# Preparing the output weights' combinations in eight smaller pieces, with their transfers on ScalarE's queue, and two reordered places on VectorE

## The chip, the cores and the metric

The kernel runs on one core of a Trainium2 chip. The metric is the device time of one launch in microseconds (us), lower is better; each version is timed several times and the median is taken. The core has five engines with an instruction queue each: TensorE (PE in the rows; its weight loads are PEld), VectorE (DVE), ScalarE (ACT), GpSimd (POOL) and SyncE (SP). Each works its queue in order; they meet at semaphores. Transfers between the memory outside the core (HBM) and its on-chip memory are issued on the queues of SP, ACT or POOL and carried by 16 shared DMA engines.

## The reference

A hybrid decoder block on 1024 tokens (plus 16 learned meta tokens) of width 1024, all in float32:

```python
h = rms_norm(z, norm_w[l])
p = (h @ w_in[l] + b_in[l])                     # 1024 -> 8 x 1024
q, fz, iv, g_hg, u, g_pool, m_hg, m_pool = split(p, 8)
o    = rms_norm(hgrn2_chunkwise(q, k, iv, log_f))
y_hg = (o * silu(g_hg)) @ w_down_hg[l]
y_pool = (mixed * pool_scale[l] * silu(g_pool)) @ w_down_pool[l]   # mixed: pooled windows @ pool_w
merged = sigmoid(m_hg) * y_hg + sigmoid(m_pool) * y_pool
z = z + merged @ w_out[l]
out = rms_norm(z, final_norm_w)
```

What matters here are the big matrix products, `h @ w_in`, the two `w_down` products, `merged @ w_out`, and the preparation of the weights `w_out`.

## The kernel before

**Products.** Every 1024-wide matrix product is cut into pairs of 128-column weight blocks, numbered p = 0 to 43. One pair is computed Strassen-Winograd fashion: seven products i = 0 to 6 instead of eight, written here as (p, i). One product is twelve matmuls (L1596): each float32 operand is split into a high part (`w_hi`, `r_hi`, made by ScalarE) and a low part (`w_lo`, `r_lo`, made by VectorE), and high x high, high x low and low x high are summed over four blocks of 128. TensorE takes the products in a fixed order, and three waits recur inside a pair: product (p, 4) needs the bank copied by `copy_second`, (p, 5) needs the copy by `copy_fifth` (ScalarE), and (p, 6) needs `add_22` (VectorE), the quarter that the fifth product ends. (p, 2) needs `copy_first`.

**Who does what beside a product.** For ScalarE and VectorE the function `during(p, i)` lists what they do beside product (p, i): ScalarE copies a bank, applies a sigmoid to a finished quarter (`extra`, L1064) and makes the high part of the weights three products ahead (`high`, L910). VectorE adds a quarter (`add_11` L1957, `add_22` L1966, `add_12` L1973), makes the low part three products ahead (`ahead`, L1872), and at i = 5 sums the next pair's weights (`weight_sums`, L1902 to L1907). All are written by hand in program order, so an instruction that waits holds everything behind it on its engine.

**Stages.** Pairs 26 and 27 (P_MM) and 28 to 31 (P_MH) make the merge gates; pairs 32 to 35 (P_DH) and 36 to 39 (P_DP) are the two down products; 40 to 43 the output product. At 31 to 32 and 35 to 36 the shared operand changes: seven operands (`r_hi`, `r_lo`, 128 x 2048 each) are replaced while products still run. VectorE's order there is the hand-written function `change(f)`: sums over the staged tiles (`stage_sum`, L2452 to L2463), low parts (`operand_low`, L2443) and the usual work. The staged tiles (`stage`) come back from HBM by four 1 MB transfers per change, issued on ScalarE's queue (`load_stage`, L1308).

**The w_out combinations.** The output product too is of the Winograd form, so four sums and differences of blocks of `w_out` have to be made (V5, V7, V6, V4). This is done ahead, during pairs 27 to 30, in one buffer `comb` of four views of 128 x 512: GpSimd issues the load of a piece (L828), VectorE makes the four sums (`comb_sums`, L2382 to L2388, in two parts after two neighbouring products, by the table `COMB_AT`), GpSimd issues the store (L833), then the next load, which waits for the store to have landed. There are four pieces of 1 MB. Load and store are placed by `COMB_DMA` between GpSimd's stores of finished gates (`store_spill`, L798). The first load waits for the last stores of the pooling part (`side_area_free`: semaphores `c_stored`). `stage_sum` of V5 at (30, 3) writes over `comb` and waits until all four pieces are stored. The buffer's memory is shared with the tile of V5.

Of the kernel before, what the change touches and what calls it, by code (L numbers as in the profile page):

```python
# [12 lines left out]
P = 128  # L13
# [40 lines left out]
def pair_table():  # L54
# [6 lines left out]
    for g in range(4):  # L61
# [76 lines left out]
COMB_AT = {(P_MM + 1, 3): (0, 0), (P_MM + 1, 4): (0, 1), (P_MH, 1): (1, 0), (P_MH, 2): (1, 1),  # L138
           (P_MH + 1, 0): (2, 0), (P_MH + 1, 1): (2, 1), (P_MH + 1, 6): (3, 0), (P_MH + 2, 0): (3, 1)}
COMB_DMA = {(P_MM, 3): -1, (P_MM + 1, 0): 0, (P_MH, 0): 1, (P_MH, 3): 2, (P_MH + 1, 3): 3}  # L140
# [45 lines left out]
def hybrid_block(nc, x, meta, norm_w, wstream, pool_w, b_in, lb_logits, hg_norm_w, pool_scale, final_norm_w, out):  # L186
    names = ExitStack()
    with names:
# [15 lines left out]
            "comb_loaded", "comb_made", "comb_stored", "out_loaded0", "out_loaded1", "out_loaded2", "out_loaded3", "out_loaded4", "out_loaded5",  # L204
# [137 lines left out]
        comb = at("comb", [P, 4, HALF], F32, work + 4 * 8192)  # L342
# [47 lines left out]

        third_begun = (S["third_begun0"], S["third_begun1"])
# [181 lines left out]
        def _(sp):  # L573
# [38 lines left out]
            def load_gate(u):  # L612

                n, t = QUARTERS[u % 4]
                after(sp, S["part_made"], u - 1)
                sp.wait_ge(spill_stored[u % 4], 16 * STORES_OF[P_MH + u // 4, u % 4])
                sp.dma_start(gate_in[u % 2][:, :], gate_dram[MH][2 * (u // 4) + n, t]).then_inc(g_loaded[u % 2], 16)
# [19 lines left out]
            def load_slot(slot):  # L637
# [5 lines left out]
                else:  # L643
                    ins = sp.dma_start(dst.rearrange("p (b k) c -> p b (k c)", b=2),
# [42 lines left out]
        def _(pool):  # L687
# [132 lines left out]
            out_blocks = wstream[2 * N_PAIRS:2 * N_PAIRS + 8].rearrange("(b s) p c -> s p b c", s=2)  # L820

            def load_comb(k):

                if k == 0:
                    side_area_free(pool)
                else:
                    pool.wait_ge(S["comb_stored"], 16 * k)
                pool.dma_start(comb[:, :, :], out_blocks[k // 2][:, :, k % 2 * HALF:(k % 2 + 1) * HALF]) \  # L828
                    .then_inc(S["comb_loaded"], 16)

            def store_comb(k):
                pool.wait_ge(S["comb_made"], k + 1)
                pool.dma_start(comb_dram[:, k // 2].rearrange("b p c -> p b c")[:, :, k % 2 * HALF:(k % 2 + 1) * HALF],  # L833
                             comb[:, :, :]).then_inc(S["comb_stored"], 16)
# [1969 lines left out]
```

## Time and profile before

| what | us |
|---|---|
| median of 3 runs | 1050.41 (1050.28 to 1050.82) |
| the profiled execution | 1051.89 |
| its span, first to last instruction | 1050.2 |
| TensorE busy, matmuls | 1018.8 (97%) |
| VectorE busy | 811.9 (77%) |
| ScalarE busy | 510.6 (49%) |
| GpSimd busy | 106.1 (10%) |
| moved by DMA | 117.17 MB, mean 112 GB/s |

Times in rows are from the start of the span. A busy share of 97% leaves little idle time on TensorE, and what there is lies in a few places, so the view to read is TensorE's own timeline: a row there is a run of matmuls with its start, its length, and in brackets how long the engine was idle before it and who released it. A row of the other engines reads the same way.

### The profile page before, as it was taken

The page shows a single profiled execution, that of the slowest core. Times are in us where ns is not written, and L with a number is a line of the kernel's source. Part 1 is how long each engine was busy: PE and PEld are TensorE (multiplying, and loading weights), DVE is VectorE, ACT ScalarE, POOL GpSimd, SP SyncE. Part 2 cuts the span into 40 slices and gives each one's busy share as a digit, 9 for nine tenths or more (in the row PEclk, how much of TensorE's full clock was granted, in tenths as well). Part 3 has the DMA queues.
Part 4 walks back from the last instruction along what each step waited for, and adds up shares of the span by engine and source line. Part 5 has one row for each costly group of instructions (what it writes and reads, how often), then busy time and mean ns, then how long its engine had stood idle before and what let it go on. Part 6 is the DMA issues. An engine that isn't in the chain of part 4 may idle for free.

```text
span 1050.2 us, 18526 instructions
## 1 busy us (share of the span) xinstructions
PE 1018.8 (97%) x7204; PEld 828.9 (79%) x7204; DVE 811.9 (77%) x1319; ACT 510.6 (49%) x860; POOL 106.1 (10%) x170
## 2 busy tenths in 40 slices
PE   7999999999999999999999999999899999999996
PEld 7767888888888888878888887787677888778885
DVE  7989787878787869696676776865468879978975
ACT  7764636363636363644353333443337536435664
POOL 6200000000000101020101001011111011000130
PEclk9999999999999999999999999999999999999999
DMA  7221111111110202121312122135773393568374
GB/s 275 51 81 62 42 61 42 62 42 61 39 64 29 74 23 81 41 101 32 101 55 96 54 78 100 51 125 197 261 293 96 120 351 128 210 204 309 84 164 125
DMA packets 40582, 117.17 MB, mean 112 GB/s; under 512 B 4752, under 2 KB 4752, under 8 KB 40496
## 3 DMA queue, kind: packets, MB, share of 16 engines
q1 hardware_dynamic: 23680, 70.33, 20.4%
q0 software_dynamic: 11152, 34.65, 10.1%
q10 hardware_dynamic: 5664, 11.02, 3.0%
q8 instruction: 57, 0.93, 0.4%
q14 instruction: 29, 0.24, 0.1%
HBM read 86.62 MB, written 29.36 MB: 110 GB/s over the span
## 4 chain that ended last, share of the span: by engine, by line
PE 61%; issue 18%; DVE 13%; DMA 4%; ACT 1%; POOL 1%; SPq 0%; ACTq 0%; DVEq 0%; POOLq 0%
PE acc L1596 49%; DMA comb<-in_wstream 2%; PE levels L1649 2%; DVE r_lo L2443 1%; DVE w_lo L1872 1%; PE miscs L1671 1%; PE miscs L1682 1%; PE miscs L1683 1%; PE acc L1538 1%; DVE att L2029 1%; PE levels L1596 1%; DVE qx L2048 1%; POOL c_spill L818 1%; DMA pt_in<-part_spill 1%; PE miscs L1689 1%
## 5 line engine op out<-in xcount | busy, mean ns | idle before, releaser
L1596 PE MATMUL acc<-r_hi,w_hi 128*128 128x512 f32 x1200 | 333.3, 399 | 11.0 <-ACT fifth L1000 3.4
L1596 PE MATMUL acc<-r_lo,w_hi 128*128 128x512 f32 x1200 | 329.2, 393 | 0.9 <-DVE r_lo L2443 0.8
L1596 PE MATMUL acc<-r_hi,w_lo 128*128 128x512 f32 x1200 | 323.0, 391 | 3.3 <-DVE w_lo L1872 3.3
L1596 PEld LDWEIGHTS acc<-r_hi,w_hi 128*128 128x128 f32 x1200 | 218.2, 188 | 61.7 <-ACT fifth L1000 4.9
L1596 PEld LDWEIGHTS acc<-r_hi,w_lo 128*128 128x128 f32 x1200 | 225.5, 188 | 52.4 <-DVE w_lo L1872 4.2
L1596 PEld LDWEIGHTS acc<-r_lo,w_hi 128*128 128x128 f32 x1200 | 223.6, 188 | 54.7 <-issue 4.9
L910 ACT ACTIVATE w_hi<-sum 128x512 fp32r<-128x512 f32 x164 | 102.8, 628 | 167.9 <-DVE sum L1905 86.0
L1872 DVE TENSOR_TENSOR w_lo<-sum,w_hi 128x512 fp32r<-128x512 f32 x164 | 111.8, 686 | 47.9 <-ACT w_hi L910 47.4
L1872 DVE TENSOR_TENSOR w_lo<-raws,w_hi 128x512 fp32r<-128x512 f32 x120 | 81.9, 686 | 45.7 <-ACT w_hi L910 45.6
L910 ACT ACTIVATE w_hi<-raws 128x512 fp32r<-128x512 f32 x120 | 74.3, 623 | 21.8 <-PE acc L1596 19.1
L1000 ACT ACTIVATE second<-acc,bias 128x512 f32<-128x512 f32 x31 | 21.2, 684 | 57.8 <-PE acc L1596 57.7
L782 POOL TENSOR_TENSOR o_rs<-o_ms,minus_half 128x8 f32<-128x8 f32 x8 | 16.0, 2003 | 306.9 <-DVE o_ms L2128 306.9
L1000 ACT ACTIVATE first<-acc,bias 128x512 f32<-128x512 f32 x32 | 22.1, 690 | 35.1 <-PE acc L1596 35.1
L1000 ACT ACTIVATE fifth<-acc,bias 128x512 f32<-128x512 f32 x31 | 21.3, 686 | 29.9 <-PE acc L1596 29.5
L2443 DVE TENSOR_TENSOR r_lo<-stage,r_hi 128x2048 fp32r<-128x2048 f32 x14 | 32.0, 2284 | 1.1 <-ACT r_hi L1329 1.1
L1907 DVE TENSOR_TENSOR sum<-sum,raws 128x512 f32<-128x512 f32 x38 | 26.3, 692 | 1.3
L818 POOL DMA_DIRECT2D c_spill<-pg x16 | 8.6, 539 | 179.7 <-DVE pg L2375 179.2
L1329 ACT ACTIVATE r_hi<-stage 128x2048 fp32r<-128x2048 f32 x14 | 26.8, 1913 | 0.0
L1905 DVE TENSOR_TENSOR sum<-sum,raws 128x512 f32<-128x512 f32 x38 | 26.0, 685 | 0.0
L1903 DVE TENSOR_TENSOR sum<-raws 128x512 f32<-128x512 f32 x38 | 26.0, 685 | 0.0
L1902 DVE TENSOR_TENSOR sum<-raws 128x512 f32<-128x512 f32 x38 | 26.0, 685 | 0.0
L1683 PE MATMUL miscs<-vv,att 128*128 128x128 f32 x128 | 24.7, 275 | 0.0
(314 smaller groups left out, 1311.2 us busy)
## 6 DMA issues: line engine op xcount, KB each, us to landing
raws<-in_wstream SPq DMA_DIRECT2D x80, 512.0 KB, 3.7
xin<-in_x SPq DMA_DIRECT2D x8, 512.0 KB, 6.2
a_spill<-gt POOLq DMA_DIRECT2D x16, 256.0 KB, 3.5
c_spill<-pg POOLq DMA_DIRECT2D x16, 256.0 KB, 2.7
comb<-in_wstream POOLq DMA_DIRECT2D x4, 1024.0 KB, 7.8
comb_spill<-comb POOLq DMA_DIRECT2D x4, 1024.0 KB, 5.5
stage<-a_spill ACTq DMA_DIRECT2D x4, 1024.0 KB, 10.7
smh_spill<-zq POOLq DMA_DIRECT2D x16, 256.0 KB, 6.3
```

The lines of the kernel that those rows point to most:

```text
L910: act.activation(high_of(o), operand(o), ACT.Copy).then_inc(S["w_hi"], 1)
L1000: return act.activation(dst, src, ACT.Identity, bias=b, scale=scale)
L1329: act.activation(r_hi[i][:, :, :], STAGED[i][:, :, :], ACT.Copy).then_inc(S["r_hi"], 1)
L1596: ins = pe.matmul(bank[:, :], weights, moving, start=n == 0 and i in (0, 1, y_first), stop=n == 3 * KH - 1, skip_group_check=True)
L1649: ins = pe.matmul(lev[g * GROUP:(g + 1) * GROUP, c * n:(c + 1) * n], kt[:, META + t.start:META + t.stop], q, start=True, stop=True)
L1683: ins = pe.matmul(dst, att[:, s], vv[:, s], start=False, stop=True)
L1872: dve.tensor_tensor(low_of(o), operand(o), high_of(o).bitcast(F32), ALU.subtract).then_inc(S["w_lo"], 1)
L1902: dve.tensor_tensor(sums[S1][:, :], a21, a22, ALU.add).then_inc(done, 1)
L1903: dve.tensor_tensor(sums[S3][:, :], a11, a21, ALU.add).then_inc(done, 1)
L1905: dve.tensor_tensor(sums[S2][:, :], sums[S1][:, :], a11, ALU.add).then_inc(done, 1)
L1907: dve.tensor_tensor(sums[S4][:, :], sums[S2][:, :], a12, ALU.add).then_inc(done, 1)
L2443: dve.tensor_tensor(r_lo[i][:, :, :], STAGED[i][:, :, :], r_hi[i][:, :, :].bitcast(F32), ALU.subtract) \
```

## The change

- The combinations are made in eight pieces of 512 KB (four views of 128 x 256) in three buffers in place of four pieces in one. Two buffers share the memory of the old one, the third lies where `gate_in` lies later.
- Loads and stores of the pieces move from GpSimd's queue to ScalarE's, at places that the tables `COMB_LOAD` and `COMB_STORE` give: after `during(p, i)` of the product named. A load waits for the store of the piece that had the buffer before it; a store waits for the sums. The sums of a piece are made whole, after one product (`COMB_SUM`).
- The four stage loads for the first change of operand, two at (28, 3) and two at (29, 3) before, are issued singly at (28, 6), (29, 3), (29, 6) and (30, 0). `stage_sum` of V5 and V7 move from (30, 3) and (30, 6) to (30, 1) and (30, 3).
- In `change`, used for both changes of operand, VectorE makes the second low part (`operand_low` of B21) and the next `ahead` before `add_22`, not after it.
- In pair 37 the first merge (`use(P_DP, ...)` of that pair's first quarter) moves from after product 4 to after product 5, so behind `add_22` and `weight_sums`.
- Two waits of SP (the first two loads of `gate_in`, and the loads of the combinations at the end) name the new semaphores.

```diff
+COMB_PIECES = 8
+COMB_BUFFER = (0, 1, 2, 0, 1, 2, 0, 2)
+COMB_LOAD = {(P_MM + 1, 1): 0, (P_MM + 1, 2): 1, (P_MM + 1, 3): 2, (P_MH, 1): 3, (P_MH, 3): 4, (P_MH, 5): 5,
...
+STAGE_LOAD = {(P_MH, 6): 0, (P_MH + 1, 3): 1, (P_MH + 1, 6): 2, (P_MH + 2, 0): 3}
...
-                    if (p, x) in COMB_DMA:
-                        k = COMB_DMA[p, x]
-                        if k >= 0:
-                            store_comb(k)
-                        if k < 3:
-                            load_comb(k + 1)
...
+            def load_comb(k):
+
+                n, turn = COMB_BUFFER[k], comb_turn(k)
+                if k == 0:
+                    side_area_free(act)
+                after(act, comb_stored[n], 16 * turn)
+                act.dma_start(comb[n][:, :, :], out_blocks[k // 4][:, :, comb_columns(k)]).then_inc(comb_loaded[n], 16)
+
+            def store_comb(k):
+                n = COMB_BUFFER[k]
+                act.wait_ge(S["comb_made"], k + 1)
+                act.dma_start(comb_dram[:, k // 4].rearrange("b p c -> p b c")[:, :, comb_columns(k)], comb[n][:, :, :]) \
+                    .then_inc(comb_stored[n], 16)
+
+            def comb_and_stage(p, i):
+
+                if (p, i) in COMB_STORE:
+                    store_comb(COMB_STORE[p, i])
+                if (p, i) in COMB_LOAD:
+                    load_comb(COMB_LOAD[p, i])
+                if (p, i) in STAGE_LOAD:
...
@@ -2500,9 +2522,9 @@
                 add_11(p)
                 ahead(p, 3)
                 use(p, 0)
-                add_22(p)
                 operand_low(f, R_B21)
                 ahead(p, 4)
+                add_22(p)
                 ahead(p, 5)
...
-                    if p == P_DH - 2 and i in (3, 6):
-                        stage_sum(0, R_V5 if i == 3 else R_V7)
+                    if p == P_DH - 2 and i in (1, 3):
+                        stage_sum(0, R_V5 if i == 1 else R_V7)
...
-                elif i == 4:
+                elif i == 5:
                     use(P_DP + 1, 0)
```

The order on VectorE beside (27, 3) to (27, 5), before; `zq_159` is the quarter of `add_22`:

```order
L1872 TENSOR_TENSOR w_lo_88<-raws,w_hi_84 128x512
L2382 TENSOR_TENSOR comb<-comb 128x512
L2383 TENSOR_TENSOR comb<-comb 128x512
L1872 TENSOR_TENSOR w_lo_85<-raws,w_hi_81 128x512
L2386 SCALAR_TENSOR_TENSOR comb<-comb 128x512
L2388 SCALAR_TENSOR_TENSOR comb<-comb 128x512
L1966 SCALAR_TENSOR_TENSOR zq_159<-acc,fifth 128x512
```

and after (line numbers are those of the new file):

```order
L1894 TENSOR_TENSOR w_lo_88<-raws,w_hi_84 128x512
L1894 TENSOR_TENSOR w_lo_85<-raws,w_hi_81 128x512
L2404 TENSOR_TENSOR comb_171<-comb_171 128x256
L2405 TENSOR_TENSOR comb_171<-comb_171 128x256
L2407 SCALAR_TENSOR_TENSOR comb_171<-comb_171 128x256
L2409 SCALAR_TENSOR_TENSOR comb_171<-comb_171 128x256
L1988 SCALAR_TENSOR_TENSOR zq_159<-acc,fifth 128x512
```

The four sums now stand together, one product later, at half the width, still ahead of `add_22`.

ScalarE beside (27, 1) to (27, 5), before; what is in square brackets are the semaphores waited for:

```order
L910 ACTIVATE w_hi_82<-sum_92 128x512 [waits mm_done,sums_made]
L910 ACTIVATE w_hi_83<-sum_93 128x512 [waits mm_done,sums_made]
L1000 ACTIVATE second<-acc,bias 128x512 [waits added,mm_done]
L1064 ACTIVATE zq_158<-zq_158 128x512 [waits added]
L910 ACTIVATE w_hi_84<-raws 128x512 [waits mm_done,raw_loaded1]
L1000 ACTIVATE fifth<-acc,bias 128x512 [waits added,mm_done]
L910 ACTIVATE w_hi_81<-raws 128x512 [waits mm_done,raw_loaded2]
L910 ACTIVATE w_hi_82<-raws 128x512 [waits mm_done,raw_loaded2]
```

and after:

```order
L901 ACTIVATE w_hi_82<-sum_92 128x512 [waits mm_done,sums_made]
L1318 DMA comb_171<-in_wstream 128x4x256 [waits c_stored2,c_stored3,c_stored1,c_stored0]
L901 ACTIVATE w_hi_83<-sum_93 128x512 [waits mm_done,sums_made]
L1318 DMA comb_172<-in_wstream 128x4x256
L991 ACTIVATE second<-acc,bias 128x512 [waits added,mm_done]
L1055 ACTIVATE zq_158<-zq_158 128x512 [waits added]
L901 ACTIVATE w_hi_84<-raws 128x512 [waits mm_done,raw_loaded1]
L1318 DMA comb_173<-in_wstream 128x4x256
L991 ACTIVATE fifth<-acc,bias 128x512 [waits added,mm_done]
L901 ACTIVATE w_hi_81<-raws 128x512 [waits mm_done,raw_loaded2]
L901 ACTIVATE w_hi_82<-raws 128x512 [waits mm_done,raw_loaded2]
L1323 DMA comb_spill<-comb_171 128x4x256 [waits comb_made]
```

Three loads and a store now stand between ScalarE's copies; the first load and every store wait there.

VectorE at the first change of operand, beside (31, 3) to (31, 5), before; `r_lo_67` is the second low part, `zq_159` the quarter of `add_22`:

```order
L1872 TENSOR_TENSOR w_lo_88<-raws,w_hi_84 128x512
L1966 SCALAR_TENSOR_TENSOR zq_159<-acc,fifth 128x512
L2443 TENSOR_TENSOR r_lo_67<-stage_151,r_hi_60 128x2048
L1872 TENSOR_TENSOR w_lo_85<-raws,w_hi_81 128x512
L1872 TENSOR_TENSOR w_lo_86<-raws,w_hi_82 128x512
```

and after:

```order
L1894 TENSOR_TENSOR w_lo_88<-raws,w_hi_84 128x512
L2464 TENSOR_TENSOR r_lo_67<-stage_151,r_hi_60 128x2048
L1894 TENSOR_TENSOR w_lo_85<-raws,w_hi_81 128x512
L1988 SCALAR_TENSOR_TENSOR zq_159<-acc,fifth 128x512
L1894 TENSOR_TENSOR w_lo_86<-raws,w_hi_82 128x512
```

`add_22` now stands behind a 128 x 2048 operation and a 128 x 512 one.

## Rows read from the trace of the kernel before

**Rows 1.** Windows: busy us of each engine, granted clock, DMA share, GB/s

```profile
740.00:765.00 25.00, 20.52 (x80) 16.04 (x79) 11.38 (x19) 8.14 (x15) 3.14 (x5) 0.86 0.76 264
```

**Rows 2.** Timeline of TensorE, 690 to 830: start, length, operation, idle before, releaser

```profile
716.93 1.21 PE L1596 MATMUL acc<-r_hi,w_hi 128*128 128x512 f32 x4 [1.04 <-DVE zq L1966]
...
735.30 1.20 PE L1596 MATMUL acc<-r_hi,w_hi 128*128 128x512 f32 x4 [1.71 <-ACT fifth L1000]
...
752.67 1.07 PE L1596 MATMUL acc<-r_lo,w_hi 128*128 128x512 f32 x4
756.51 2.08 PE L1596 MATMUL acc<-r_hi,w_lo 128*128 128x512 f32 x4 [2.78 <-DVE w_lo L1872]
760.28 2.08 PE L1596 MATMUL acc<-r_hi,w_hi 128*128 128x512 f32 x4 [1.70 <-ACT fifth L1000]
762.16 1.60 PE L1596 MATMUL acc<-r_lo,w_hi 128*128 128x512 f32 x4
763.59 1.07 PE L1596 MATMUL acc<-r_hi,w_lo 128*128 128x512 f32 x4
764.50 1.07 PE L1596 MATMUL acc<-r_hi,w_hi 128*128 128x512 f32 x4
...
785.33 1.20 PE L1596 MATMUL acc<-r_hi,w_hi 128*128 128x512 f32 x4 [1.63 <-DVE zq L1966]
```

**Rows 3.** Timeline of VectorE, the same stretch

```profile
705.82 0.69 DVE L1957 TENSOR_TENSOR zq<-acc,first 128x512 f32<-128x512 f32 x1 [1.55 <-DMA c_spill<-pg]
...
713.05 0.69 DVE L2382 TENSOR_TENSOR comb<-comb 128x512 f32<-128x512 f32 x1 [2.83 <-DMA comb<-in_wstream]
...
731.20 0.69 DVE L2382 TENSOR_TENSOR comb<-comb 128x512 f32<-128x512 f32 x1 [6.52 <-DMA comb<-in_wstream]
...
754.56 0.69 DVE L2382 TENSOR_TENSOR comb<-comb 128x512 f32<-128x512 f32 x1 [11.25 <-DMA comb<-in_wstream]
...
781.78 2.29 DVE L2452 TENSOR_TENSOR stage<-stage,stage 128x2048 f32<-128x2048 f32 x1 [1.64 <-DMA comb_spill<-comb]
```

**Rows 4.** Issues by line, 690 to 800, and their landing: weights (512 KB), stage (1 MB)

```profile
L581 SPq DMA_DIRECT2D raws<-in_wstream x9: 327/328/328, 694.5 to 788.4; - x9
...
DMA to landing us min/median/max: 3.3/5.7/8.7
...
L1308 ACTq DMA_DIRECT2D stage<-a_spill x4: 366/460/541, 733.5 to 758.9; - x4
...
DMA to landing us min/median/max: 6.1/10.7/14.0
```

**Rows 5.** Timeline of ScalarE: two rows of its work

```profile
711.08 0.62 ACT L910 ACTIVATE w_hi<-raws 128x512 fp32r<-128x512 f32 x1
...
734.56 0.69 ACT L1000 ACTIVATE fifth<-acc,bias 128x512 f32<-128x512 f32 x1 [0.28 <-issue]
```

**Rows 6.** Timelines of VectorE and TensorE at the first change of operand

```profile
801.07 0.69 DVE L1872 TENSOR_TENSOR w_lo<-raws,w_hi 128x512 fp32r<-128x512 f32 x1 [1.22 <-ACT w_hi L910]
802.04 0.69 DVE L1966 SCALAR_TENSOR_TENSOR zq<-acc,fifth 128x512 f32<-128x512 f32 x1 [0.28 <-PE acc L1596]
...
804.50 1.07 PE L1596 MATMUL acc<-r_hi,w_hi 128*128 128x512 f32 x4
...
826.80 1.20 PE L1596 MATMUL acc<-r_lo,w_hi 128*128 128x512 f32 x4
```

**Rows 7.** The same two timelines at the second change of operand

```profile
879.78 0.69 DVE L1966 SCALAR_TENSOR_TENSOR zq<-acc,fifth 128x512 f32<-128x512 f32 x1 [0.56 <-issue]
...
882.24 1.07 PE L1596 MATMUL acc<-r_hi,w_hi 128*128 128x512 f32 x4
...
906.35 1.21 PE L1596 MATMUL acc<-r_lo,w_hi 128*128 128x512 f32 x4
```

**Rows 8.** The same two timelines in pair 37

```profile
922.41 0.69 DVE L2479 TENSOR_TENSOR mm<-mm,sp_in 128x512 f32<-128x512 f32 x1 [1.26 <-DMA pt_in<-part_spill]
...
924.49 1.19 PE L1596 MATMUL acc<-r_hi,w_hi 128*128 128x512 f32 x4 [0.58 <-DVE mm L1966]
```

More of the change, by code:

```diff
@@ L339, in hybrid_block @@
         m = [mm[:, n, :] for n in range(NK)]
-        comb = at("comb", [P, 4, HALF], F32, work + 4 * 8192)
+        comb = [at(f"comb{n}", [P, 4, HALF // 2], F32, place)
+                for n, place in enumerate((work + 4 * 8192, work + 4 * 8192 + 4096, side + 8192))]
         out_sums = [at(f"out_sum{n}", [P, HALF], F32, ring_at + RING * 4096 + 2048 * n) for n in range(4)]
@@ L389, in hybrid_block @@
         comb_dram = nc.dram_tensor("comb_spill", [4, 2, P, D], F32, kind="Internal").ap()
+        comb_loaded = tuple(S[f"comb_loaded{n}"] for n in range(3))
+        comb_stored = tuple(S[f"comb_stored{n}"] for n in range(3))
         third_begun = (S["third_begun0"], S["third_begun1"])
@@ L643, in load_slot @@
                 else:
+                    for n in range(3):
+                        sp.wait_ge(comb_stored[n], 16 * COMB_BUFFER.count(n))
                     ins = sp.dma_start(dst.rearrange("p (b k) c -> p b (k c)", b=2),
@@ L1309, in load_stage, with comb_columns, comb_turn @@
                     .then_inc(stage_loaded[n // 2], 16)
+            out_blocks = wstream[2 * N_PAIRS:2 * N_PAIRS + 8].rearrange("(b s) p c -> s p b c", s=2)
+            def comb_columns(k):
+                lo = k % 4 * (HALF // 2)
+                return slice(lo, lo + HALF // 2)
+            def comb_turn(k):
+                return COMB_BUFFER[:k].count(COMB_BUFFER[k])
+            def load_comb(k):
[15 more added lines that the diff above has]
+                if (p, i) in STAGE_LOAD:
+                    if STAGE_LOAD[p, i] == 0:
+                        for x in range(4):
+                            act.wait_ge(spill_stored[x], 16 * STORES_OF[P_MM, x])
+                    load_stage(0, STAGE_LOAD[p, i])
             for p in range(P_POOL, P_MH):
@@ L1333, in _ @@
                     during(p, i)
-                    if p in (P_MH, P_MH + 1) and i == 3:
-                        if p == P_MH:
-                            side_area_free(act)
-                            for x in range(4):
-                                act.wait_ge(spill_stored[x], 16 * STORES_OF[P_MM, x])
-                        load_stage(0, 2 * (p - P_MH))
-                        load_stage(0, 2 * (p - P_MH) + 1)
-                    elif p in (P_DH - 1, P_DP - 1) and i in (1, 2, 4, 5):
+                    comb_and_stage(p, i)
+                    if p in (P_DH - 1, P_DP - 1) and i in (1, 2, 4, 5):
                         operand_high((p + 1 - P_DH) // 4, i - 1 if i < 3 else i - 2)
@@ L2375, in mixed, with comb_sums @@
                 dve.tensor_tensor(v, mix_banks[k], v, ALU.mult).then_inc(S["c_made"], 1)
-            def comb_sums(k, part):
-                v5_, v4_, v7_, v6_ = (comb[:, n, :] for n in range(4))
-                dve.wait_ge(S["comb_loaded"], 16 * k + 16)
-                if part == 0:
-                    steps.mark(dve.tensor_tensor(v5_, v5_, v7_, ALU.subtract))
-                    steps.mark(dve.tensor_tensor(v7_, v6_, v7_, ALU.subtract))
-                    return
+            def comb_sums(k):
+                n = COMB_BUFFER[k]
+                v5_, v4_, v7_, v6_ = (comb[n][:, v, :] for v in range(4))
+                dve.wait_ge(comb_loaded[n], 16 * (COMB_BUFFER[:k].count(n) + 1))
+                steps.mark(dve.tensor_tensor(v5_, v5_, v7_, ALU.subtract))
+                steps.mark(dve.tensor_tensor(v7_, v6_, v7_, ALU.subtract))
                 steps.settle()
```

36 lines of the change are left out of this document (15 added, 21 removed).

## The prediction, made before the changed kernel ran

> **What bounds the kernel now.** I read TensorE's own timeline first, since its work fills the span. In steady work a batch of four matmuls is shown as 1.07 long, but batches start 0.91 apart (763.59 and 764.50), so a product of three batches takes 2.72 [rows 2]. The sum of its matmuls doesn't change here; only its stops can. Between 690 and 830 there are five that the change aims at: idle 1.04, 1.71, 2.78, 1.70 and 1.63, sum 8.86 [rows 2]. The full price of a stop is more than its idle time. The last batch before it doesn't overlap the next (1.07 - 0.91 = 0.16, five times: 0.8), and the first one after it takes 1.20 or 1.21 in place of 1.07 (three times: 0.4). At 756.51 the clock falls as well: after 2.78 idle two batches take 2.08 and one 1.60 (excess 1.01 + 1.01 + 0.53 = 2.55), and the granted clock of 740 to 765 is 0.86 on average, where it otherwise stands at the higher level, 2.4 GHz; batches that take twice as long are batches at 1.2 GHz [rows 1, 2]. All together: 8.86 + 0.8 + 0.4 + 2.55 = **12.6 us**.
>
> Then I asked who is late. VectorE's timeline gives it: it stood still for the load of a piece for 2.83, 6.52 and 11.25 us, and at 781.78 for 1.64 us for the last store, each shortly before a stop [rows 3]. Three of the stops name ScalarE or w_lo: the fifth's copy (735.30, 760.28) was late because ScalarE's queue held a sigmoid that waited for VectorE's add. So all five have one cause: in one buffer, load, sums, store and next load follow one another, and VectorE waits for them in order, ahead of an add that TensorE needs.
>
> **Part 1: eight pieces, three buffers, ScalarE's queue.** Everything before 705.8 stays; the first load still waits for the pooling part's last stores, as VectorE does until 705.82 [rows 3]. I lay the new order over a TensorE that doesn't stop and look at whether every step is in time.
>
> - *The sums.* An operation of 128x512 takes 0.69, one of 128x2048 takes 2.29 [rows 3], so 512 elements more cost 0.53, and one of 128x256 should take 0.69 - 0.27 = 0.42. The trace has no such operation; bounds are 0.35 (half) and 0.69 (no gain). A piece is four: 1.7 us, at most 2.8. Eight pieces are 13.6, four of before were 4 x 4 x 0.69 = 11.0: 2.6 us more on VectorE, which idled some 22 us for pieces.
> - *Piece 0.* ScalarE issues it at about 705.9. VectorE's turn: the w_hi at 711.08 ends at 711.7 [rows 5], its low part follows, so the sums can begin at 712.3. Their latest start: (27, 6) is due at 716.93 - 1.04 - 0.16 = 715.7; a release acts 0.74 after the operation's start (734.56 to 735.30 [rows 2, 5]), so `add_22` must start by 715.0 and the sums by 713.3. The load may take 7.4 us.
> - *Pieces 3 and 6* are the others whose sums stand at i = 4, just ahead of an `add_22`. Each is issued behind ScalarE's work at (p, 1), about 0.85 after that product starts; (p, 6) starts 5 x 2.72 = 13.6 after (p, 1), less 0.74 and 1.7: 11.15. Allowed: 10.3 us.
> - *The remaining pieces* have sums at i = 6, 1 or 2's border; behind them stand low parts needed three products later and `copy_first`, with 1.5 us or more in hand on top of 8 to 14 us for the load.
> - *What a load takes.* Nearest in bytes are the weights' loads, 512 KB: 3.3, median 5.7, at most 8.7. Nearest in queue and shape are the stage loads (ScalarE, many rows, twice the bytes): 6.1, 10.7, 14.0 [rows 4]. I take 5.7, for the same bytes: every piece is in time, piece 0 with 1.7 us to spare. The ends are 3.3 and 14.0.
> - *ScalarE.* 16 transfers are added on its queue; the four stage loads were there already. An issue takes 0.37 to 0.54 [rows 4], mostly beside an operation still running: two in a row left 0.28 idle at 734.56 [rows 5]. Each costs ScalarE 0 to 0.5 us, and it's idle half the time. What waits behind a store's wait (for the sums) are `copy_first` at (28, 0) and (29, 0): the sums there end about 0.9 before that copy's own turn, and TensorE needs the copy 1.8 after it. Cost zero; without this cover, 0.5 each. GpSimd loses eight issues and their waits; its gate stores go out sooner.
> - *The stage loads and sums.* The last load is issued at (30, 0), some 12 us before `add_22` of pair 30 must start. Behind it V7's operation (2.2) and one low part (0.6) must fit: of 15.3 us between the issue (about 757.6, on the new timeline) and (30, 6) at 772.9, less 0.74, 0.6 and 2.2, 11.7 are left. The median 10.7 fits, the longest, 14.0, doesn't (2.3 late) [rows 4]. V5 waits for stores issued more than 8 us earlier. Nothing waits for the sums themselves before `change`.
>
> So the five stops go: **-12.6**.
>
> **Part 2: the order at operand changes.** At the first, VectorE waits 0.28 for TensorE before `add_22`, and that add starts 0.97 after the low part before it, where operations back to back start 0.60 apart (the 0.69 of one overlap a little): 0.37 us are open [rows 6]. In the new order the 128x2048 low part fills this. The price: `add_22` starts behind it and one low part, at about 804.47 in place of 802.04, and releases TensorE at 805.21, which began (31, 6) at 804.50 without idling [rows 6]: a new stop of 0.71, and 0.13 for the restart. Is it lost? VectorE's timeline has no other gap from here to the last low part, and TensorE's batch at 826.80, a low x high one with the 1.20 of a restart, starts on that part [rows 6]: the end of the change is set by VectorE. TensorE's new stop is time that it would have stood later anyway. So -0.35, not +0.8. At the second change, idle is 0.56 ahead of the same add, some 0.65 with the overlap; the add now starts at 879.78 - 0.65 + 2.2 + 0.6 = 881.93, and the new stop is 881.93 + 0.74 - 882.24 = 0.43, and VectorE again releases TensorE at the end, at 906.35 [rows 7]. **-0.35 and -0.6.**
>
> **Part 3: pair 37.** VectorE waits 1.26 us for `pt_in`, and `add_22` stands behind; TensorE idles 0.58 before (37, 6), then 0.16 and 0.12 as above [rows 8]. Moved ahead of the merge, the add is in time: **-0.85**. The merge comes about 2 us later, and with it SP's next load, whose user is six operations on; TensorE isn't near it.
>
> Sum: 12.6 + 0.35 + 0.6 + 0.85 = 14.4. The profiled execution took 1051.89 (span 1050.2), 1.5 more than the median; a difference carries over, so 1050.41 - 14.4 = **1036.0**.
>
> **The skill against the trace.** The Trainium skill, "DMA: Bandwidth & Descriptors", section "Bandwidth", advises transfers of 1 MiB or more and gives 2.0 us plus bytes over 436 GB/s for one. An estimate by this page: 3.2 us for 512 KB and 4.4 us for 1 MB, so sixteen small transfers cost 51 us where eight large ones cost 35. It speaks against cutting them, and if they ran one by one the sum would be 16 us worse. The rows show 3.3 to 8.7 for 512 KB [rows 4], in keeping as a floor. The same page, "Why small descriptors are slow (HBM only)", counts three cycles per packet on top of 32-byte beats; as an estimate, rows of 1 KB would cost 35/32 against 67/64 for rows of 2 KB, 4.5% more. No run here has shown it yet.
>
> **Rivals.**
> - *Some pieces late.* Transfers queue behind one another: gates' stores, weights, 1 MB stage loads on the same queue. With piece 0 at 8.7 us it is 1.3 late, V7 at 14.0 is 2.3 late, plus 0.3 for each restart: 4.2 us given back, **1040.2**. For it: 14.0 has occurred. Against: three buffers allow 7.4 to 14 us.
> - *The reorder isn't given back.* Should something other than VectorE end the changes, TensorE's new stops stay (0.84 + 0.56) and the gains (0.95) don't come: 1036.0 + 2.35 = **1038.4**. Against: the rows at 826.80 and 906.35.
> - *Slower: small rows make every piece as slow as a stage load.* If a row of 1 KB costs the DMA engines what a row of 2 KB costs, a piece of 512 KB is as slow as 1 MB, and both engines that TensorE depends on stop, VectorE for the load and ScalarE for the sums. At 14.0 each, piece 0 is 6.6 late, 3 and 6 are 3.7, V7 is 2.3: 16.3, and the low clock after two stops adds 2 x 2.55: 21.4, so **1057.4**. It decides from about 12 us per piece. For it: the queue's own rows (median 10.7); against: those are twice the bytes. The advice of the page on 1 MiB would lead here, and its three cycles per packet away from it.
>
> **How the numbers follow.** Forecast 1036.0: 0.60, its own range 1034.6 to 1037.6 (small stops before 830 that I left out could go too: low end). Late pieces, 1037.6 to 1043: 0.23. Reorder not given back: 0.10. Slower: 0.06; no change 0.01. Range 1034.6 to 1041.0, which leaves out some 0.15. Faster by over 0.2% (about what a measurement of this kernel tells from no change): 0.93; within: 0.01; slower: 0.06.
>
> **What would show it.** Of the profile after: no idle over 0.5 on TensorE between 700 and 790, its clock at the high level there, VectorE's waits for `comb` near zero in place of 28; pieces landing in 4 to 8 us; (30, 6) at about 772.9; a new idle of about 0.7 before (31, 6) and 0.4 before (35, 6), each with `add_22` as releaser, and the changes ending 0.35 and 0.6 earlier against TensorE's start of pair 31 and 35; no stop at (37, 6). Wrong is: VectorE still waiting at i = 4 for pieces 0, 3 or 6, a wait for stage before V7, or a copy on ScalarE held up by a store's wait.

## The result, and the profile after

| | before | changed |
|---|---|---|
| median | 1050.35 us (1049.14 to 1050.82, 4 runs) | 1037.73 us (1037.35 to 1038.02, 4 runs) |
| ratio | 1 | 0.9881 [0.9864, 0.9899] |
| profiled execution, span | 1051.89, 1050.2 | 1037.68, 1035.5 |

The changed kernel is faster by 12.6 us; 1036.0 was forecast (1034.6 to 1041.0). From the page of the profile after: the span, the engines' busy time, the queues (packets, MB, share of the 16 engines; q0 is GpSimd's, q10 ScalarE's) and the group of matmuls on which most stops had lain, with its count, busy us, mean ns, and the idle time before it:

```profile
span 1035.5 us, 18554 instructions
...
PE 1013.8 (98%) x7204; PEld 827.2 (80%) x7204; DVE 813.8 (79%) x1335; ACT 510.5 (49%) x860; POOL 100.3 (10%) x162
...
q0 software_dynamic: 8976, 26.26, 8.0%
q10 hardware_dynamic: 14112, 19.41, 5.4%
...
L1618 PE MATMUL acc<-r_hi,w_hi 128*128 128x512 f32 x1200 | 331.8, 398 | 4.4 <-ACT second L991 1.7
```

The same lines of before; the idle time ahead of that group falls from 11.0 to 4.4:

```profile
q0 software_dynamic: 11152, 34.65, 10.1%
q10 hardware_dynamic: 5664, 11.02, 3.0%
...
L1596 PE MATMUL acc<-r_hi,w_hi 128*128 128x512 f32 x1200 | 333.3, 399 | 11.0 <-ACT fifth L1000 3.4
```

The window that answers to [rows 1], same columns. TensorE is busy all through 25 us, with 112 matmuls (28 batches) in place of 80, and the granted clock is at the higher level, 1.00 where it was 0.86:

```profile
740.00:765.00 25.00, 25.00 (x112) 20.71 (x111) 16.40 (x29) 10.60 (x18) 2.16 (x4) 1.00 1.02 363
```

TensorE's timeline (start, length, operation, idle before and its releaser), answering to [rows 2, 6 and 7]. Between 690 and 790 there's no idle at all. The product (30, 6), which began at 785.33 after a stop of 1.63 before, starts at 772.60; the first stop after the sums of the pieces is the one before (31, 6), then (35, 6) at 869.67:

```profile
772.60 1.07 PE L1618 MATMUL acc<-r_hi,w_hi 128*128 128x512 f32 x4
775.32 1.07 PE L1618 MATMUL acc<-r_hi,w_hi 128*128 128x512 f32 x4
...
792.35 1.20 PE L1618 MATMUL acc<-r_hi,w_hi 128*128 128x512 f32 x4 [0.52 <-DVE zq L1988]
813.56 1.19 PE L1618 MATMUL acc<-r_lo,w_hi 128*128 128x512 f32 x4
...
869.67 1.20 PE L1618 MATMUL acc<-r_hi,w_hi 128*128 128x512 f32 x4 [0.41 <-DVE zq L1988]
...
892.68 1.20 PE L1618 MATMUL acc<-r_lo,w_hi 128*128 128x512 f32 x4
```

VectorE's timeline, answering to [rows 3]: the first operation of pieces 0 and 3, which stand just ahead of an `add_22`, and V7's sum. None has a wait in brackets, where the four pieces of before had cost 2.83, 6.52, 11.25 and, at 773.79, 7.39:

```profile
712.09 0.42 DVE L2404 TENSOR_TENSOR comb<-comb 128x256 f32<-128x256 f32 x1
...
731.13 0.42 DVE L2404 TENSOR_TENSOR comb<-comb 128x256 f32<-128x256 f32 x1
...
767.36 2.28 DVE L2478 TENSOR_TENSOR stage<-stage,stage 128x2048 f32<-128x2048 f32 x1
```

The issues of the pieces and the landing of loads and stores together, answering to [rows 4]:

```profile
L1318 ACTq DMA_DIRECT2D comb<-in_wstream x8: 374/384/664, 705.4 to 752.3; - x8
...
L1323 ACTq DMA_DIRECT2D comb_spill<-comb x8: 366/366/373, 713.8 to 762.8; - x8
...
DMA to landing us min/median/max: 2.8/5.3/9.4
```

Of the loads alone it is 3.6, 6.2 and 9.4 (forecast 3.3 to 14.0, taken 5.7). The group has no engine that waits for `comb`.

### The profile page after: what moved, and what is told of

Same layout as the page of the kernel before. It is cut to its first block, busy times and chain, and to the rows that moved or that the text cites. A ratio compares the mean times of both kernels' runs of the same rounds, so it can differ in the third digit from the quotient of the medians.

```text
span 1035.5 us, 18554 instructions
## 1 busy us (share of the span) xinstructions
PE 1013.8 (98%) x7204; PEld 827.2 (80%) x7204; DVE 813.8 (79%) x1335; ACT 510.5 (49%) x860; POOL 100.3 (10%) x162
## 3 DMA queue, kind: packets, MB, share of 16 engines
q0 software_dynamic: 8976, 26.26, 8.0%
## 4 chain that ended last, share of the span: by engine, by line
PE 81%; DVE 13%; issue 3%; ACT 2%; DMA 1%; POOL 0%; DVEq 0%; SPq 0%; ACTq 0%
PE acc L1618 67%; PE levels L1671 2%; DVE w_lo L1894 1%; PE miscs L1693 1%; PE miscs L1705 1%; PE miscs L1704 1%; DVE r_lo L2464 1%; PE acc L1560 1%; PE miscs L1500 1%; PE levels L1500 1%; DVE att L2051 1%; PE levels L1618 1%; DVE qx L2070 1%; PE miscs L1711 1%; PE miscs L1684 1%
## 6 DMA issues: line engine op xcount, KB each, us to landing
stage<-a_spill ACTq DMA_DIRECT2D x4, 1024.0 KB, 10.1
```

## Experiments

All times are medians beside runs of the kernel before on the same chip (1050.11 for the first four, 1050.49 for the second four, 1050.22 for the last four, 13 runs each). Numbers 1, 6 and 11 have 10 runs, the others 4. The intervals of the ratio are 2 to 3 us wide, and the changed kernel itself gave 1037.73 and 1037.02; so versions that differ by about 1 us aren't told apart by their medians, and there the distances in the traces carry the argument.

A measure is used that needs no end of the kernel: TensorE's restart at about 665 (0.59 idle, in all kernels, ahead of everything that is changed) to the start of (30, 6). Before, from the rows: 785.33 - 665.55 = 119.78. After: 772.60 - 665.29 = 107.31.

### 1. The kernel before, again

No edit.

> The kernel before, unchanged, to see how far one profiled execution of it stands for the others. The span of the changed kernel fell by 14.7 us in its profile, as the steps said, but its median by only 12.6. Theory A (the five stops between 700 and 830 depend on when transfers land, and the profiled execution had long ones): this execution's span is near 1048.5, with 10.5 to 11.5 us lost in the stops in place of 12.6, most of the difference at the third stop with its low clock. Theory B (the stops are the same every time, and the difference lies outside the span): the span is 1050 again, the loss 12.6, and the time outside the span is not the 1.7 us of the first profile but smaller.

Measured: 1050.24, ratio 0.9998 [0.9989, 1.0008], profiled span 1049.2. TensorE's stops in this execution:

```profile
716.47 1.19 PE L1596 MATMUL acc<-r_hi,w_hi 128*128 128x512 f32 x4 [1.06 <-DVE zq L1966]
734.17 1.20 PE L1596 MATMUL acc<-r_hi,w_hi 128*128 128x512 f32 x4 [1.07 <-ACT fifth L1000]
755.63 1.23 PE L1596 MATMUL acc<-r_hi,w_lo 128*128 128x512 f32 x4 [3.04 <-DVE w_lo L1872]
759.40 2.07 PE L1596 MATMUL acc<-r_hi,w_hi 128*128 128x512 f32 x4 [2.55 <-ACT fifth L1000]
784.48 1.19 PE L1596 MATMUL acc<-r_hi,w_hi 128*128 128x512 f32 x4 [1.10 <-DVE zq L1966]
...
923.57 1.19 PE L1596 MATMUL acc<-r_hi,w_hi 128*128 128x512 f32 x4 [0.26 <-DVE mm L1966]
```

The same five places, other sizes: 1.71 at 735.30 in [rows 2] is 1.07 here, 1.70 at 760.28 is 2.55, and 0.58 at pair 37 [rows 8] is 0.26. The stop near 735 follows the landing of the second piece: VectorE waited 6.52 for it in the first trace, 5.88 here and 5.05 in number 6, and TensorE then stood 1.71, 1.07 and 0.24, each time less by the same amount. To (30, 6) it took 119.41; in two further kernels that leave this stretch alone (numbers 6 and 11) 118.57 and 118.63. The execution I forecast from was at the slow end. This one trace lies between the two theories (0.4 less lost, where A expected 1.1 to 2.1 less); it's numbers 6 and 11, 1.2 less each, that bear out A, and the third stop isn't where the difference lies (2.78 and 3.04).

### 2. The combinations alone

```diff
                 use(p, 0)
+                add_22(p)
                 operand_low(f, R_B21)
                 ahead(p, 4)
-                add_22(p)
...
-                elif i == 5:
+                elif i == 4:
                     use(P_DP + 1, 0)
```

> The changed kernel with both reorderings undone: add_22 stands ahead of the second low part again, and the merge of pair 37 stands after product 4. My theory: the eight pieces bring nearly everything; 1.8 us of the forecast 14.4 are missing, so about 1.8 us slower than the changed kernel (1039.5), with no stop on TensorE between 700 and 790, none before (31, 6), (35, 6) and (36, 6)'s end as in the kernel before, and the stop of 0.58 before (37, 6). Rival (the reorder is not given back, but costs): this kernel is as fast as the changed one or faster at the two changes of operand by up to 1.4 us, and only pair 37 shows a loss of 0.85.

Measured: 1038.83, ratio 0.9890 [0.9875, 0.9905]. No stop from 690 to 790, (30, 6) after 107.29. Both changes of operand take as long as before (below). So the combinations carry nearly all of the gain. It is 1.1 above the changed kernel, where 1.8 was expected: the stop at pair 37 isn't there, though its edit is undone: `add_22` releases TensorE just in time. VectorE's wait for `pt_in` is there, as long as ever:

```profile
908.53 0.69 DVE L2501 TENSOR_TENSOR mm<-mm,sp_in 128x512 f32<-128x512 f32 x1 [1.20 <-DMA pt_in<-part_spill]
```

### 3. The pieces on GpSimd's queue

```diff
-                    comb_and_stage(p, i)
...
+                    for step in COMB_POOL.get((p, x), ()):
+                        (load_comb if step > 0 else store_comb)(abs(step) - 1)
```

All else (eight pieces, three buffers, the singly issued stage loads) stays.

> Eight pieces and three buffers as in the changed kernel, but all 16 transfers on GpSimd's queue, placed between its stores of finished gates; all else as in the changed kernel. Theory (the buffers are the cause, not the queue): no load is late by more than 1 us, TensorE has no or one short stop between 700 and 790, time within 1.5 us of the changed kernel's. Rival (the queue matters: a GpSimd issue takes longer, and a store that waits for the sums holds back gate stores and the next load, or ScalarE waits for a gate's buffer): 3 to 8 us slower than the changed kernel, with stops that name add_22 or the fifth's copy.

Measured: 1037.29, ratio 0.9876 [0.9861, 0.9891]: no slower than the changed kernel. One small stop is left, before (30, 6), at 107.94:

```profile
773.28 1.19 PE L1618 MATMUL acc<-r_hi,w_hi 128*128 128x512 f32 x4 [0.48 <-DVE zq L1988]
```

It isn't a piece that is late there but the stage load for V7's sum, which stands on VectorE just ahead of that `add_22`:

```profile
769.73 2.29 DVE L2478 TENSOR_TENSOR stage<-stage,stage 128x2048 f32<-128x2048 f32 x1 [2.25 <-DMA stage<-a_spill]
```

Which queue issues the pieces doesn't matter here. That the buffers do is what number 5 asks.

### 4. The stage loads in pairs, as before

```diff
-STAGE_LOAD = {(P_MH, 6): 0, (P_MH + 1, 3): 1, (P_MH + 1, 6): 2, (P_MH + 2, 0): 3}
+STAGE_LOAD = {(P_MH, 3): (0, 1), (P_MH + 1, 3): (2, 3)}
```

> The changed kernel with the four 1 MB stage loads issued in two pairs, at (28, 3) and (29, 3), as in the kernel before. Theory (the load on the DMA engines around 730 to 752 is what comes nearest to making pieces late): behind 2 MB of stage loads the store of piece 3 and the loads of pieces 5 and 6 land 4 to 6 us later; piece 6 has 10.3 us and is late by 0 to 2, ScalarE also waits for the store of piece 3 before it loads piece 6; time 0.5 to 3 us above the changed kernel's. Rival (pieces have room enough, the stage loads' places don't matter): same time within 0.3 us, no stop between 700 and 790.

Measured: 1038.74, ratio 0.9889 [0.9874, 0.9903], 1.0 above the changed kernel's 1037.73. Two stage loads queued together make two pieces late, and two stops come back. VectorE's waits, then TensorE's:

```profile
744.37 0.43 DVE L2405 TENSOR_TENSOR comb<-comb 128x256 f32<-128x256 f32 x1 [2.43 <-DMA comb<-in_wstream]
...
764.20 0.42 DVE L2405 TENSOR_TENSOR comb<-comb 128x256 f32<-128x256 f32 x1 [3.22 <-DMA comb<-in_wstream]
```

```profile
770.50 1.19 PE L1619 MATMUL acc<-r_hi,w_hi 128*128 128x512 f32 x4 [0.36 <-ACT fifth L991]
774.06 1.20 PE L1619 MATMUL acc<-r_hi,w_hi 128*128 128x512 f32 x4 [0.54 <-DVE zq L1989]
```

To (30, 6) it is 108.91, 1.6 more. 5.7 us of waiting on VectorE cost TensorE 0.9 us of idle. On ScalarE the copy `second` waits twice, 7.1 in all, behind a store that waits for the late sums.

### 5. Two buffers in place of three

```diff
-COMB_BUFFER = (0, 1, 2, 0, 1, 2, 0, 2)
+COMB_BUFFER = (0, 1, 0, 1, 0, 1, 0, 1)
```

with the loads moved to the first place at which their buffer's store has been issued.

> The changed kernel with two buffers in place of three, filled in turn; loads are issued as early as the store before them allows: (27, 1), (27, 2), (27, 6), (28, 2), (28, 3), (28, 6), (29, 2), (29, 4). Sums and stores stand where they do in the changed kernel. A load now has 5 to 8 us before its sums in place of 8 to 14. Theory (room for the load is what removes the stops): landings of 5 to 10 us make pieces 3 and 6 late by up to 2 us each and ScalarE waits for stores; 0.5 to 4 us slower than the changed kernel. Rival (overlapping one load with one set of sums is enough): same time within 0.3 us.

Measured: 1045.37, ratio 0.9954 [0.9939, 0.9969], 7.6 above the changed kernel: more than I gave for it. The waits (engine, line, what for: us in total, times, longest) name the cause, and it isn't a late load:

```profile
DVE stage L2474 <- DMA comb_spill<-comb: 6.4, 1, 6.4
ACT second L991 <- DMA comb_spill<-comb: 5.6, 1, 5.6
```

```profile
750.12 1.21 PE L1618 MATMUL acc<-r_hi,w_hi 128*128 128x512 f32 x4 [1.64 <-ACT second L991]
776.00 2.07 PE L1618 MATMUL acc<-r_hi,w_hi 128*128 128x512 f32 x4 [3.79 <-ACT fifth L991]
```

A load that waits on ScalarE's queue for its buffer's store holds the copy `second` behind it for 5.6 us. And V5's sum overwrites the memory of buffers 0 and 1: with the last piece in buffer 1 it has to wait 6.4 us for that piece's store. The last stop is followed by batches of 2.07, those at 1.2 GHz. (30, 6) comes after 115.68, 8.4 late.

So two causes lie together in this run: loads that wait for stores, and the last piece in V5's memory. The changed kernel puts its last piece into buffer 2, outside that memory. No run has two buffers with the last piece elsewhere, or with the loads off ScalarE's queue, so how the 7.6 divides is open.

### 6. The order alone

Everything as before, pair 37 too; only `add_22` stands, at both changes of operand, where the changed kernel has it.

> The kernel before with the one reorder at both changes of operand: second low part and one low part of weights ahead of add_22. Theory (VectorE sets the end of a change, so TensorE's new stop is time it would have stood later): new stops of about 0.7 before (31, 6) and 0.4 before (35, 6), yet from the start of (31, 0) to the batch released by the last low part 0.35 to 0.4 less than 38.62, and from the start of (35, 0) 0.5 to 0.65 less than 40.43; time 0.9 below the kernel before. Rival (not given back): these distances grow by 0.3 to 0.8, the time rises by 1 to 1.4. A second sample of the five stops before 830 as well.

Measured: 1048.89, ratio 0.9986 [0.9976, 0.9995]; its spans have a median of 1047.2, those of before on the same chip 1048.7. That's 1.6 less where 0.9 was expected; the interval (0.5 to 2.5) covers both. Now the changes of operand, as the distance on TensorE from the first batch of pair 31 (after: 775.32) to the batch that the last low part releases (813.56), and the same at pair 35 (852.77 to 892.68):

| | first change | second change |
|---|---|---|
| before; before again | 38.62; 38.62 | 40.44; 40.43 |
| combinations alone | 38.63 | 40.43 |
| order alone | 38.25 | 39.89 |
| changed; changed again | 38.24; 38.23 | 39.91; 39.90 |

Whoever has the new order gains 0.38 and 0.53, and nobody else. TensorE's new stops of 0.52 and 0.41 lie inside these distances. What they are given back from can be seen too: before, TensorE stood at two later places inside the same distances, and neither stop is there in the changed kernel:

```profile
813.55 1.20 PE L1596 MATMUL acc<-r_hi,w_hi 128*128 128x512 f32 x4 [0.73 <-ACT first L999]
896.14 1.19 PE L1596 MATMUL acc<-r_lo,w_hi 128*128 128x512 f32 x4 [0.40 <-DVE r_lo L2443]
```

### 7. `add_22` directly behind the second low part

```diff
                 operand_low(f, R_B21)
-                ahead(p, 4)
                 add_22(p)
+                ahead(p, 4)
```

> The changed kernel with add_22 directly behind the second low part, so ahead of the low part of the next weights. Theory (VectorE is busy without a gap up to the end of the change, so the order inside it doesn't move the end): the stop of 0.52 before (31, 6) shrinks below 0.1 and that before (35, 6) goes, but the batch that waits for the last low part starts at the same distance from (31, 0) and (35, 0), 38.24 and 39.90, within 0.1; time the same. Rival (TensorE's stop is real loss): both distances shrink by 0.5 to 0.7, time 1.0 to 1.3 lower.

Measured: 1037.10, ratio 0.9876 [0.9861, 0.9891]. The stops before (31, 6) and (35, 6) are gone, and the first change takes 38.24 all the same. This shows that the first stop was never a loss: VectorE sets the end of the change. The second change takes 39.54, 0.36 less than the 39.90 expected. That isn't the order either. From VectorE's gate multiplication at the start of pair 35 to the batch that the last low part releases it is 39.77 in the changed kernel (852.91 to 892.68) and 39.78 here (852.30 to 892.08). VectorE only came to it earlier, 0.24 before (35, 0) in place of 0.14 behind it, and it comes there straight from its waits for the landings of `gate_in` in pair 34 (the last one 0.50 here, 0.82 in the changed kernel).

### 8. Two gate multiplications behind the last low part

Number 7, and at the second change:

```diff
-                use(p, 2)
...
-                use(p, 3)
...
+                use(p, 2)
+                use(p, 3)
```

> The kernel of add_second in which, at the second change of operand, two gate multiplications of pair 35 (0.6 each) move behind the last low part. Theory: VectorE sets the pace of the change through its low parts, so these come 0.6 and 1.2 earlier, and the batch released by the last one starts about 1.1 nearer to (35, 0): 38.8 in place of 39.90; what follows is SP's load for the merge, which waits for all parts, with 0.9 of room; time 0.6 to 1.2 below add_second. Rival (the load comes late and VectorE waits for it in pair 37): the gain is lost at (37, 6), time the same or up to 1.5 higher.

Measured: 1036.64, ratio 0.9874 [0.9859, 0.9888]. The second change takes 38.71, so 38.8 came true; the time is 0.5 below number 7, where 0.6 to 1.2 was expected.

### 9 and 10. The changed kernel and number 8 on one chip

> The changed kernel, unchanged, for a comparison on the same chip with the kernel that has the late parts. Expected: 1037.7, 12.6 below before, and spans between 1035 and 1036.

> The kernel with the late parts (at the change of operand the quarter of the fifth product directly behind the second low part, and at the second change two gate multiplications behind the last low part), again. If the shift of 1.2 us at the second change is real and lasts to the end, it is 0.6 to 1.2 us below the changed kernel: 1036.5 to 1037.1. If its new stop of 0.56 before (34, 6) eats it, the two are equal within 0.3 us.

Measured: 1037.02, ratio 0.9878 [0.9863, 0.9893], and 1037.07, 0.9876 [0.9861, 0.9890]. They are equal. The second change is again 1.2 shorter (38.70), but TensorE's timeline of number 10 has two stops that the changed kernel's hasn't:

```profile
850.25 1.20 PE L1618 MATMUL acc<-r_hi,w_hi 128*128 128x512 f32 x4 [0.30 <-DVE zq L1988]
889.62 1.19 PE L1618 MATMUL acc<-r_hi,w_hi 128*128 128x512 f32 x4 [0.61 <-DVE mm L1988]
898.78 1.20 PE L1618 MATMUL acc<-r_hi,w_hi 128*128 128x512 f32 x4 [0.32 <-ACT first L990]
```

(the middle one is in both). By the prediction's price of a stop, idle time plus 0.16 and 0.12, they cost 0.58 and 0.60, which is all of the 1.2. The one at 898.78 lies just behind the change. The one at 850.25, before (34, 6), lies ahead of the multiplications that were moved, where VectorE had waited 1.35 for `gate_in`; (34, 6) is late in the changed kernel as well, 850.29 in number 9 with a batch of 1.20. So it follows a landing, and no run ties it to the edit. The first 1036.64 was no evidence for a better kernel.

### 11. Four more semaphores

The kernel before, with four names more in its list of semaphores, which nothing uses.

> The kernel before with four more semaphores, which nothing uses, as many as the eight pieces brought. All else is equal, so the span stays that of before (1048.5, give or take 1). Theory: the time outside the span, 1.75 us before and 2.1 in every kernel with the eight pieces, grows with the count of semaphores, 2.1 here. Rival: it goes with the transfers, 1.75 here.

Measured: 1050.17, ratio 1.0001 [0.9992, 1.0011]. The time outside the span is 1.75, that of before. The theory has fallen.

### 12. Before, with each piece's transfers cut in two

```diff
-                pool.dma_start(comb[:, :, :], out_blocks[k // 2][:, :, k % 2 * HALF:(k % 2 + 1) * HALF]) \
-                    .then_inc(S["comb_loaded"], 16)
+                for lo in (0, HALF // 2):
+                    pool.dma_start(comb[:, :, lo:lo + HALF // 2],
+                                   out_blocks[k // 2][:, :, k % 2 * HALF + lo:k % 2 * HALF + lo + HALF // 2]) \
+                        .then_inc(S["comb_loaded"], 16)
```

and the stores likewise; four pieces, one buffer, GpSimd's queue.

> The kernel before, with each load and store of a piece of the combinations issued as two transfers of 512 KB with rows of 1 KB, on GpSimd's queue, still into one buffer and with four pieces. Two questions. Cost of a 1 KB row: my theory (the queue table of the changed kernel: about 5% dearer per byte) expects the share of GpSimd's queue to rise from 10.1% by about 0.1 of a point, and the time to stay within 2 us of before, since the chain of load, sums, store and next load keeps its length. The rival of the prediction, a row of 1 KB as dear as one of 2 KB, expects that queue's share to rise by some 2.5 points and the pieces to land twice as late. Time outside the span: if it grows by 0.4 us here as it did with the eight pieces (1.75 to 2.1), it goes with the number or shape of the transfers; if it stays at 1.75, it goes with something else of that part.

Measured: 1059.60, ratio 1.0091 [1.0076, 1.0106]. I had expected no change; it is 9.4 us slower. VectorE's waits, beside [rows 3]:

```profile
729.71 0.69 DVE L2386 TENSOR_TENSOR comb<-comb 128x512 f32<-128x512 f32 x1 [4.96 <-DMA comb<-in_wstream]
754.12 0.69 DVE L2386 TENSOR_TENSOR comb<-comb 128x512 f32<-128x512 f32 x1 [12.31 <-DMA comb<-in_wstream]
776.77 0.69 DVE L2386 TENSOR_TENSOR comb<-comb 128x512 f32<-128x512 f32 x1 [10.07 <-DMA comb<-in_wstream]
788.21 2.29 DVE L2456 TENSOR_TENSOR stage<-stage,stage 128x2048 f32<-128x2048 f32 x1 [5.10 <-DMA comb_spill<-comb]
```

From the issue of a load to the sums is 6.95, 6.44, 7.57 and 7.53 (before 6.92, 9.94, 6.86, 8.74): the loads are no slower. From the issue of a store to its successor (next load, or V5's sum at the end) is 6.58, 12.73, 11.60 and 7.19, in sum 38.1, before 4.69, 12.38, 6.97 and 4.47, in sum 28.5. So it's the stores: 9.6 more, 4.0 less for the loads, 5.6 of the 6.3 by which the chain from the first load to V5's sum grows. TensorE then stands 5.71 before (30, 6), after 126.14, and has batches at 1.2 GHz behind it:

```profile
791.76 2.07 PE L1600 MATMUL acc<-r_hi,w_hi 128*128 128x512 f32 x4 [5.71 <-DVE zq L1970]
793.63 1.91 PE L1600 MATMUL acc<-r_lo,w_hi 128*128 128x512 f32 x4
```

Why a store in two halves lands later is open: the second half is issued 0.75 later, and the third store's second half at about 758.4, just behind two stage loads (758.06), where the whole store had gone out ahead of them before (758.08 against 758.51); no run took these apart. The packets speak against the rows as the reason. GpSimd's queue here:

```profile
q0 software_dynamic: 11280, 34.65, 10.2%
```

Before it was 11152 packets and 10.1%: 128 more, which is 16 for each of the eight transfers more, and not thousands. The small rows on this queue don't become small packets, and the price of 1 KB rows wasn't tested by this kernel as I had meant it to be.

## Why the prediction was right, and where it wasn't

**The stops and their price.** Right in the place, close in the size. From the trace I used, 12.6 were to go; (30, 6) came at 107.31 in place of 119.78, so 12.5 went. From the landings of a typical execution less is to be had: the four traces with the old combinations give 119.78, 119.41, 118.57 and 118.63, mean 119.1, so 11.8. That is the mis-sized term, 0.8 too much. Even with that, the reading holds that a stop costs more than its idle time: in number 11 the five stops idle 7.7 and (30, 6) comes 11.3 later than in the changed kernel. (The prediction's 22 us of idling on VectorE leave out the 7.39 for the fourth piece, its 28 has it; no term rests on either.)

**Pieces in time.** Right. Pieces landed in 3.6 to 9.4 and VectorE never waited for one. Number 4 shows how little there was in hand: stage loads issued in pairs suffice for 5.7 us of waiting. The rival of late pieces didn't come about; spreading the stage loads, of which I had made no term, is what keeps it away, worth 1.6 on the way to (30, 6) and 1.0 in the median. Its other half, V7's sum late, was nearer: no wait in the first trace of the changed kernel, but 0.5 in the second, 0.3 in number 2 and 2.25 in number 3. The two small ones cost TensorE nothing, the last 0.48 of idle. By the prediction's own list such a wait is a sign of being wrong: its allowance of 11.7 for that load has little to spare.

**The sums.** An operation took 0.42 (416 to 427 ns), as estimated. ScalarE's issues took 0.37 to 0.66, and the first load stood behind work that waited for the pooling part's stores anyway; no copy was late.

**Three buffers.** I argued with the loads' time only. Numbers 5 and 12 complete the picture of the cause: the old kernel's trouble was load, sums, store and next load in one line, and the stores' part of it (28.5) is nearly as large as the loads' (32.5). Cut transfers in one buffer: +9.4. Eight pieces in two buffers: -5.1. In three: -12.6 and -13.2. Two things stay untested: whole pieces of 1 MB in more than one buffer, so what the smaller size brings by itself, and the earlier places of V5's and V7's sums, which every kernel with eight pieces has.

**The order at the changes.** Right: 0.38 and 0.53 gained (forecast 0.35 and 0.6), and the stops are where they were forecast, 0.52 and 0.41 idle for 0.71 and 0.43. The forecast of a stop was reckoned from when the product would else have begun, and a row counts idle time only from the end of the batch before it, 0.16 later. Reckoned the first way, (31, 6) starts 17.03 behind (31, 0) in place of 16.32, so 0.71 later, just as forecast, and (35, 6) 16.90 behind (35, 0) in place of 16.32, so 0.58 for 0.43. The rival, not given back, is refuted by the table and by number 7.

**Pair 37.** The step that failed. I booked 0.85 for a stop of 0.58 that another execution of the same kernel has at 0.26, and that numbers 2, 6, 11 and 12 don't have at all, though none of them has this edit. What decides is the landing of `pt_in`: VectorE starts the merge 6.01 behind `add_11` of pair 37 in the trace I used, 5.66 in number 1, and 4.90 to 5.14 in those four. Worth 0 to 0.85, it should have stood in the range and not in the sum. No run has this edit alone. Changed and combinations alone differ by 0.75 to 1.0 behind (30, 6) (262.9 and 263.1 against 263.9), which the changes of operand cover by themselves (0.91).

**From the trace to the median.** "A difference carries over" was too simple. The profiled span fell by 14.7, the median by 12.6. The spans of the kernel before have a median of 1048.5 in its other runs (1047.2 to 1049.9), so the profiled one, 1050.2, was 1.7 above; that is the luck of the stops and of pair 37. And the time outside the span went from 1.75 to about 2.1 in every kernel with the eight pieces: 14.7 - 1.7 - 0.4 = 12.6. Numbers 11 and 12 show that the 0.4 isn't in four more semaphores (1.75) nor in sixteen transfers on GpSimd's queue (1.75). What it is stays open. Term by term, against a typical execution: 11.8 for the stops, 0.9 for the changes and nothing for pair 37, less the 0.4, make 12.3; 12.6 was measured. That 1036.0 lies 1.7 below the result is the stops' 0.8, pair 37's 0.85 and the 0.4, with 0.3 the other way.

**Slower by small rows.** The rival's premise is refuted: 512 KB in rows of 1 KB landed in a median of 6.2, where the stage loads of 1 MB on the same queue took 9.7 to 10.6. The queues say the same: ScalarE's went from 3.0% of 1050.2 to 5.4% of 1035.5, +24.4 us, and GpSimd's from 10.1% to 8.0%, -23.2 us, for the same 8.39 MB. That's 5% dearer, though each share is rounded to 0.05%, so that each difference is uncertain by up to 1.0 us, 4% of itself; the changed kernel against number 3 gives 9% in the same way (24.9 and 22.8). ScalarE's queue did get 8448 packets more, 8192 for the rows of 1 KB and 16 for each of the 16 transfers. The Trainium skill, "DMA: Bandwidth & Descriptors", section "Why small descriptors are slow (HBM only)", gives three cycles for each packet; the 5 to 9% are in keeping with that and with the 4.5% estimated from it, but not sharp enough to prove it. Its advice in "Bandwidth" to move 1 MiB or more at once would have led away from a gain of 12.6 us: sixteen small transfers cost TensorE nothing, since their time lies beside other work in other buffers. Where they don't overlap (number 12), cutting costs 9.4, which is in keeping with the advice, though why the cut stores land later is open. The formula that the prediction puts under "Bandwidth", 2.0 us and the bytes over 436 GB/s, stands in the Trainium skill's same page in the section "Anatomy of one DMA — SWDGE (gpsimd) path", so for a transfer of GpSimd's queue; number 3, on that queue, shows 5.3 to 8.7 for 512 KB, where the prediction's estimate from it is 3.2.

## What to carry to other kernels

When an engine in order waits for a transfer ahead of something that the bounding engine needs, count the whole round of a buffer, load, use, store, next load; in these runs smaller transfers helped with more buffers to overlap them and cost time in one, and a store that a load or an overwriting operation waits for counts as much as the load. On the engine that doesn't bound, put work into its gap even if it delays the release of the bounding one, as long as the gap-filler is what both wait for at the end. Before adding up a trace's stops, look at the same kernel in a second trace: a stop that a landing decides is a range, not a term.

## What the runs showed of the hardware

- Executions of one unchanged kernel differ by up to 3.0 us in span (1047.2 to 1050.2), and the traces tie it to stops whose length follows DMA landings (0.24 to 1.71 near 735 in kernels alike up to there, behind waits of 5.05 to 6.52 for a load).
- On GpSimd's queue 8.39 MB make as many packets with rows of 1 KB as with rows of 2 KB, apart from 16 for each transfer: 8976 packets without these transfers, 11152 with eight of them and 11280 with sixteen, so 2048 of 4 KB both times; on ScalarE's queue the rows of 1 KB gave 8192 packets, and 16 more for each transfer.
- After stops of 2.78, 2.85, 3.79, 3.83 and 5.71 the next batch took 2.07 or 2.08 in place of 1.07, so it ran at the low level of the clock, 1.2 GHz. After stops of 3.04 and 3.20 it took 1.23 and 1.19, and the batch behind the following stop (2.55 and 2.58) took 2.07.
